# A Conformer-convolution and sparse-attention step on one core: first tile's projections feature by feature, samples' value products turned round, four square buffers

## The chip, the cores and the metric

The kernel runs on one core of a Trainium2 chip. The metric is the device time of one launch, in microseconds (us); the time before is the median of three runs. A core has TensorE (PE; its weight loads are shown as PEld), VectorE (DVE), ScalarE (ACT), GpSimd (POOL) and SyncE (SP, which issues the transfers), each with its own instruction stream, and they meet through semaphores. TensorE writes to PSUM, which has eight banks of 512 fp32 values per partition.

## What is computed

Two layers with a final RMSNorm, for 512 prompt tokens and 8 samples of 4 new tokens each (544 tokens in all, model width 1024).

```python
# layer 0: convolution mixer (width 2048, 31 taps per channel)
h = rms_norm(x, norm_g[0])
a, gl, z = split(h @ w_in, 3)
v = a * sigmoid(gl)
c = silu(layer_norm(depthwise_conv(concat(buf, v), dw_w) + dw_b))
x = x + (c * silu(z)) @ w_out
# layer 1: attention with three branches (compressed, selected, window), ALiBi slopes
q, z, kv, gates = split(rms_norm(x, norm_g[1]) @ w_in)
for each branch: o += gate * softmax(q k^T * scale - slope * distance) v
x = x + (o * silu(z)) @ w_out
y = rms_norm(x, final_norm_g)
```

A sample attends to 256 past tokens (pages for the selected branch, a window buffer for the window branch), to the compressed blocks of them, and to the new tokens.

## The kernel before, in words

**Layout.** Activations are feature-major: feature on the partitions, 544 tokens along the row; X holds eight such slices of 128 features. An fp32 product is split: weights and activations are each cut into a rounded high part (ScalarE's copy to fp32r) and the rest (a subtraction on VectorE or GpSimd), and `split_product` (L563) adds high x high, high x low and low x high, each over two column halves of 256 and 288: six matmuls.

**Opening.** ScalarE squares the eight slices of x, TensorE sums them with a matrix of ones, VectorE forms the inverse root, and `spread` (L549) spreads it over all partitions into banks 0 to 3, one quarter of the tokens in each. VectorE multiplies slice k by it (L1263, counted by h_ready); ScalarE copies the high part Hh (L1036, h1h_ready); VectorE subtracts to get Xl (L1267, h1l_ready). Meanwhile ScalarE copies and GpSimd subtracts the three weight blocks of tile 0 (`high_wA` L1028, `low_wA` L1703). TensorE waits for all eight h_ready (L608), since its first results go to banks 0 and 1, from which VectorE still reads.

**Convolution, 16 tiles of 128 channels.** `tile` on TensorE (L597): project the gate, add the taps of the tile before (`add_taps`, L586), project the linear part, project z. ScalarE takes the sigmoid from PSUM and prepares the next tile's high weights; VectorE multiplies into VP and runs 19 of the 31 taps; SP writes four shifted copies of VP to G (`spread_taps`, L437), from which TensorE adds the other 12 as products with diagonal matrices that GpSimd makes; GpSimd also does the samples' convolution and subtracts the weights. In the last tile TensorE takes 24 taps, and VectorE 7.

**Normalisation and output product.** After the last tile TensorE sums C over the channels, VectorE centres the 16 slices (L1329), ScalarE squares them into two buffers (L1083), TensorE sums (L627). Then, in a pipeline: VectorE scales, ScalarE applies SiLU, GpSimd multiplies with silu(z) (L1737), ScalarE and VectorE split the result, and TensorE adds blocks 0 and 1 of the output slice by slice (L644). Blocks 2 to 7 follow one by one. Of the output weights ScalarE copies the high parts (L1077, `high_wC` L1086); GpSimd subtracts for blocks 0 and 1 (L1732), VectorE for 2 to 7 (`low_wC`, L1347). Block 2's copy and subtraction stand after the pipeline.

**Attention.** Key, value, query and gate projections, the prompt's attention, then the samples' (L958 to L974): a loop of 16 steps, in each of which TensorE computes scores of unit v (`sample_scores`, L888: 32 columns of queries as weights, each sample's keys moving), transposes the weights of unit v-2, multiplies with the values for unit v-3 (`sample_pv`, L920) and does a quarter of a block of the prompt's output product (`out2`, 2 matmuls of 512 columns). There are 12 units: 4 of the compressed and 4 of the selected branch, alternating, then 4 of the window. In `sample_pv` the values (128x128) are the weights and 32 columns of attention weights move, one product for each sample and each half of its keys, so that the result is feature-major; the sum over branches lies in OS, and `sample_gate` (L1613) multiplies it into ZT. Every fp32 matmul shows as two records in the trace. After the loop come output blocks 4 to 7 and the final norm.

Each engine's order is written out by hand; a wait blocks all that follows on its engine.

## Time and profile before

| what | value |
|---|---|
| median of three runs | 1059.06 us (1058.37 to 1059.90) |
| the profiled execution's own time | 1058.09 us |
| its span in the trace | 1056.0 us |
| TensorE busy | 986.1 us, 93% |
| VectorE, ScalarE, GpSimd busy | 649.7, 404.6, 386.6 us |

The profile names a source line and tiles for every instruction. "Idle before" is the time that an engine stood still ahead of an instruction, with what ended the wait. The chain is followed back from the last instruction to what released each step. A busy TensorE need not run at full speed: the granted clock (PEclk) is 1.00 at 2.4 GHz and 0.50 at 1.2 GHz.

### The profile page before, as it was taken

Reading aid. Unit: us, or ns where it says so; the run is one execution under the profiler, and the core shown is the slowest. Engines: PE = TensorE matmul, PEld = TensorE weight load, DVE = VectorE, ACT = ScalarE, POOL = GpSimd, SP = SyncE. Lnnn points to the kernel's source line nnn. Section 1 sums busy time; section 2 is a strip of 40 time slices with the busy share of each in tenths; the row PEclk is TensorE's granted clock in tenths of the full one; section 3 lists DMA queues with packets and bytes.
Section 4 is the critical chain, followed back from the end, with each engine's and each line's share of the span. In section 5 each row is a group of like instructions: output and inputs, shape, how many; then the busy total and the mean of one; then the engine's idle time right before and its main releaser. Section 6 shows DMA issues by size and latency. Waiting matters only on the chain.

```text
span 1056.0 us, 19270 instructions
## 1 busy us (share of the span) xinstructions
PE 986.1 (93%) x7168; PEld 836.4 (79%) x7168; DVE 649.7 (62%) x1399; ACT 404.6 (38%) x794; POOL 386.6 (37%) x328
## 2 busy tenths in 40 slices
PE   2999999999999959999899998999699999999996
PEld 0989998998899729998799678999577777756684
DVE  4498999899989679320751312344888888833103
ACT  5333334333334276221331111244577777711001
POOL 2487888788878658001010000000333333100000
PEclk9999999999999959999899999998799999999796
DMA  8243453355334450360255015211630000260002
GB/s 342 75 128 101 127 174 103 101 139 163 101 105 137 139 202 1 120 238 7 115 152 133 1 26 221 80 61 41 205 124 1 0 1 1 104 235 1 1 1 85
DMA packets 43016, 108.01 MB, mean 102 GB/s; under 512 B 20674, under 2 KB 21730, under 8 KB 38530
## 3 DMA queue, kind: packets, MB, share of 16 engines
q1 hardware_dynamic: 42946, 106.99, 31.2%
q8 instruction: 54, 0.88, 0.3%
q14 instruction: 16, 0.13, 0.0%
HBM read 81.87 MB, written 12.17 MB: 89 GB/s over the span
## 4 chain that ended last, share of the span: by engine, by line
PE 82%; DVE 7%; issue 4%; ACT 4%; POOL 3%; DMA 0%; DVEq 0%; ACTq 0%
PE ps L567 52%; PE ps L953 7%; PE ps L593 4%; PE ps L843 4%; POOL C L1737 3%; PE ps L731 2%; PE ps L831 2%; PE ps L939 1%; PE ps L545 1%; DVE SX L1527 1%; DVE KL L1496 1%; PE ps L820 1%; PE ps L795 1%; DVE X L1263 1%; PE ps L822 1%
## 5 line engine op out<-in xcount | busy, mean ns | idle before, releaser
L567 PE MATMUL ps<-Hh,ringAh 128*128 128x256 f32 (+1 forms) x768 | 161.2, 291 | 14.3 <-DVE X L1263 14.3
L567 PE MATMUL ps<-Hh,ringAl 128*128 128x256 f32 (+1 forms) x768 | 159.4, 289 | 0.0
L1307 DVE SCALAR_TENSOR_TENSOR acc<-VP,tapc,acc 128x512 f32<-128x512 f32 x122 | 159.1, 1304 | 0.0
L567 PE MATMUL ps<-Xl,ringAh 128*128 128x256 f32 (+1 forms) x768 | 158.1, 287 | 0.0
L1706 POOL TENSOR_TENSOR ringAl<-ringA,ringAh 128x1024 fp32r<-128x1024 f32 x48 | 121.1, 2535 | 73.3 <-ACT ringAh L1029 73.2
L567 PEld LDWEIGHTS ps<-Hh,ringAh 128*128 128x128 f32 x768 | 123.3, 189 | 27.2 <-DVE X L1263 14.6
L567 PEld LDWEIGHTS ps<-Xl,ringAh 128*128 128x128 f32 x768 | 124.1, 189 | 0.0
L567 PEld LDWEIGHTS ps<-Hh,ringAl 128*128 128x128 f32 x768 | 123.0, 189 | 0.0
L1307 DVE SCALAR_TENSOR_TENSOR ps<-VP,tapc,ps 128x512 f32<-128x512 f32 x138 | 102.8, 745 | 0.6
L843 PE MATMUL ps<-PTB,V 128*128 128x512 f32 (+3 forms) x256 | 91.0, 439 | 2.5 <-ACT PTB L1206 2.1
L567 PE MATMUL ps<-Hh,ringEh 128*128 128x256 f32 (+1 forms) x384 | 84.2, 302 | 7.1 <-DVE ringEl L1373 4.6
L1029 ACT ACTIVATE ringAh<-ringA 128x1024 fp32r<-128x1024 f32 x48 | 50.7, 1060 | 87.9 <-PE ps L567 83.4
L567 PE MATMUL ps<-Hh,ringEl 128*128 128x256 f32 (+1 forms) x384 | 82.5, 298 | 0.0
L567 PEld LDWEIGHTS ps<-Hh,ringEh 128*128 128x128 f32 x384 | 64.9, 199 | 8.1 <-issue 8.0
L1373 DVE TENSOR_TENSOR ringEl<-ringE,ringEh 128x1024 fp32r<-128x1024 f32 x22 | 27.4, 1248 | 67.8 <-ACT ringEh L1112 67.7
L567 PEld LDWEIGHTS ps<-Hh,ringEl 128*128 128x128 f32 x384 | 64.7, 198 | 0.0
L1773 POOL CAST QS<-QT 64x512 fp32r (+1 forms) x16 | 10.1, 629 | 146.1 <-PE ps L822 82.6
L1678 POOL TENSOR_TENSOR prod<-VS,tapc 128x248 f32<-128x248 f32 x64 | 62.1, 1006 | 3.5 <-DVE VS L1292 3.5
L567 PE MATMUL ps<-Ch,ringCh 128*128 128x256 f32 (+1 forms) x256 | 54.9, 296 | 6.5 <-ACT Ch L1099 5.1
L1684 POOL TENSOR_TENSOR prod<-prod 128x512 f32<-128x512 f32 (+1 forms) x64 | 57.7, 901 | 5.0
L1206 ACT ACTIVATE PTB<-ps 128x128 f32<-128x128 f32 (+3 forms) x128 | 53.9, 421 | 9.9 <-PE ps L831 9.9
L843 PEld LDWEIGHTS ps<-PTB,V 128*128 128x128 f32 x256 | 44.0, 188 | 16.0 <-ACT PTB L1206 8.9
(233 smaller groups left out, 2059.6 us busy)
## 6 DMA issues: line engine op xcount, KB each, us to landing
ringA<-in_w_a SPq DMA_DIRECT2D x16, 1536.0 KB, 7.3
G<-VP SPq DMA_DIRECT2D x60, 260.0 KB, 4.8
ringE<-in_w_f SPq DMA_DIRECT2D x24, 512.0 KB, 3.6
ringC<-in_w_c SPq DMA_DIRECT2D x8, 1024.0 KB, 5.9
cache_cmp<-in_cache_cmp SPq DMA_DIRECT2D x32, 128.0 KB, 2.8
cache_sel<-in_cache_sel SPq DMA_DIRECT2D x16, 256.0 KB, 3.0
cache_win<-in_cache_win SPq DMA_DIRECT2D x1, 4096.0 KB, 15.2
out_win_s<-in_win_state SPq DMA_DIRECT2D x1, 4032.0 KB, 18.1
```

Source lines behind the costliest of these rows:

```text
L567: mm = nc.tensor.matmul(dst, w, x[:, cols], start=begins, stop=ends)
L593: mm = nc.tensor.matmul(ps[32 * j:32 * j + 32, 6], d[:, j, :], G[:, j, NSH * q:NSH * q + NP_], start=(q == 0), stop=(q == len(diags) - 1))
L843: mm = nc.tensor.matmul(out[:, P * k:NP_], V[:, k, v:v + P], PTB[:, b, k, P * k:NP_], start=False, stop=(b == 1 and k == 3))
L953: mm = nc.tensor.matmul(dst, w_o(n)[:, k, :], ZT[:, k, cols], start=(k == 0), stop=(k == KT - 1))
L1029: nc.scalar.activation(ringAh[:, j], ringA[:, par, j], ACT.Copy).then_inc(wAh_ready, 1)
L1206: nc.scalar.activation(PTB[:, turn, 0:t + 1, P * t:P * t + P], ps[:, 4 + u % 2, 0:(t + 1) * P].rearrange("p (k q) -> p k q", q=P), ACT.Cop ...
L1307: nc.vector.scalar_tensor_tensor(tap_sum(k % 2), src, w, tap_sum(k % 2), ALU.mult, ALU.add).then_inc(conv_step, 1)
L1373: nc.vector.tensor_tensor(ringEl[:, n % 3], ringE[:, n % 3], ringEh[n % 2][:].bitcast(F32), ALU.subtract).then_inc(wEl_ready, 1)
L1678: op = nc.gpsimd.tensor_tensor(dst, win, w, ALU.mult)
L1684: nc.gpsimd.tensor_tensor(prod[:, 0:n, :], prod[:, 0:n, :], prod[:, n:2 * n, :], ALU.add).then_inc(pool_step, 1)
L1706: nc.gpsimd.tensor_tensor(ringAl[:, par, j], ringA[:, par, j], ringAh[:, j].bitcast(F32), ALU.subtract).then_inc(wAl_ready, 1)
L1737: nc.gpsimd.tensor_tensor(C[:, c, :], C[:, c, :], Z1[:, c, :], ALU.mult).then_inc(c_gated, 1)
```

## The change

- **First tile.** The inverse root is spread into banks 6 and 7, two quarters in each, with a wait between the two halves; VectorE reads it as two rows of 272. TensorE no longer waits for all of h_ready: for each feature slice, once its high and low parts are there, it takes the gate's and then the linear product; z follows as before. GpSimd's third weight subtraction waits for six slices of Xl.
- **Last tile.** Strips 2 and 3 of the shifted rows are issued by ScalarE's queue, ahead of its copy into acc; SP issues 0 and 1.
- **Normalisation.** Squares go to four buffers (sqc) in memory that VP and sig have left.
- **Output weights.** Block 2's copy and subtraction move to GpSimd, behind those of blocks 0 and 1.
- **Samples.** In the value products the attention weights (32 columns per sample) become the weights of the matmul and the values move (128 columns); four samples write to four groups of 32 PSUM rows. The new tokens' product is one matmul for all samples in either branch. OS then is token-major; `sample_turn` transposes each of its four tiles on TensorE, one per step from step 12 on, and `sample_gate` reads the result from PSUM.

The diff, without the declarations of the semaphores half_spread and os_t:

```diff
@@ -142,6 +142,7 @@
         Cl = at("Cl", [P, CT, T], G0, F32R)
+        sqc = at("sqc", [P, 4, T], RINGA + 2 * 3 * KT * P * 4 + 17408)
@@ -434,13 +437,13 @@
-            def spread_taps(c, par, ptaps=PTAPS):
+            def spread_taps(c, par, ptaps=PTAPS, strips=range(NCG)):
...
                 k0, width = TAPS - ptaps, NP_ + ptaps - NSH
-                for j in range(NCG):
+                for j in strips:
@@ -454,7 +457,7 @@
             spread_taps(CT - 2, 0)
-            spread_taps(CT - 1, 1, PTAPS_LAST)
+            spread_taps(CT - 1, 1, PTAPS_LAST, range(0, 2))
@@ -558,7 +561,16 @@
             pe.wait_ge(rstd_kept, 1)
-            spread(0, rstd4).then_inc(rstd_ready, 1)
+            for half in range(2):
+                for b in range(2):
+                    j = 2 * b + half
+                    mm = nc.tensor.matmul(ps[:, 6 + b, Q * half:Q * half + Q], ones[32 * j:32 * j + 1, :],
+                                          rstd4[32 * j:32 * j + 1, :], start=True, stop=True)
+                    if half == 0:
+                        mm.then_inc(half_spread, 1)
+                if half == 0:
+                    pe.wait_ge(half_spread, 2)
+            mm.then_inc(rstd_ready, 1)
@@ -570,9 +582,6 @@
                 for k in range(KT):
-                    if j == 0 and not reaches(c, 1):
-                        pe.wait_ge(h1h_ready, k + 1)
-                        pe.wait_ge(h1l_ready, k + 1)
@@ -605,8 +614,22 @@
                 project(c, par, 2, 2, z_done)
-            pe.wait_ge(h_ready, KT)
-            for c in range(CT):
+            def first_tile():
+                for k in range(KT):
+                    pe.wait_ge(h1h_ready, k + 1)
+                    pe.wait_ge(h1l_ready, k + 1)
+                    for j in range(2):
+                        if k == 0:
+                            pe.wait_ge(wAl_ready, j + 1)
+                        mm = split_product(halves(j), ringAh[:, j, k, :], ringAl[:, 0, j, k, :],
+                                           Hh[:, k, :], Xl[:, k, :], k == 0, k == KT - 1)
+                        if k == KT - 1:
+                            mm.then_inc(gate_done if j == 0 else lin_done, 1)
+                project(0, 0, 2, 2, z_done)
+            first_tile()
+            for c in range(1, CT):
@@ -624,7 +647,7 @@
                 pe.wait_ge(squared, KT + c + 1)
-                add_up(0, sq[:, c % 2], c == 0, c == CT - 1).then_inc(sq_summed, 1)
+                add_up(0, sqc[:, c % 4], c == 0, c == CT - 1).then_inc(sq_summed, 1)
@@ -650,8 +673,10 @@
                 pe.wait_ge(wCh_ready, n + 1)
-                pe.wait_ge(wCl_ready, n - 1)
-                if n >= 3:
+                if n == 2:
+                    pe.wait_ge(wCl_first, 3)
+                else:
+                    pe.wait_ge(wCl_ready, n - 2)
@@ -926,25 +951,27 @@
                 out = ps[:, 4 + m % 2]
+                if m >= 6:
+                    pe.wait_ge(og_sample, m - 5)
                 if br == 0:
-                    nc.tensor.matmul(out[:, 0:P], vcs[:, gp * P:(gp + 1) * P], PT[:, v % 2, 0:P],
+                    nc.tensor.matmul(out[:, 0:P], PT[:, v % 2, 0:P], vcs[:, gp * P:(gp + 1) * P],
...
                 vnew = (br - 1) * GROUPS * HD + gp * P
-                for q in range(4):
-                    s_, cols = 4 * sg + q, slice(32 * q, 32 * q + 32)
-                    for c in range(2):
+                for c in range(2):
+                    for q in range(4):
+                        s_ = 4 * sg + q
...
                                 else cache_win[:, s_, (2 + c) * PAST + gp * P:(2 + c) * PAST + gp * P + P])
-                        nc.tensor.matmul(out[:, cols], vals, PT[:, v % 2, P * c + 32 * q:P * c + 32 * q + 32],
+                        nc.tensor.matmul(out[32 * q:32 * q + 32, 0:P], PT[:, v % 2, P * c + 32 * q:P * c + 32 * q + 32], vals,
                                          start=(br == 2 and c == 0), stop=False)
-                    if br == 2:
-                        mm = nc.tensor.matmul(out[:, cols], V[0:NS_, 4, vnew:vnew + P],
-                                              PT[0:NS_, v % 2, PAST + 32 * q:PAST + 32 * q + 32], start=False, stop=True)
-                if br == 1:
-                    mm = nc.tensor.matmul(out[:, 0:P], V[0:NS_, 4, vnew:vnew + P], PT[0:NS_, v % 2, PAST:PAST + P],
-                                          start=False, stop=True)
-                mm.then_inc(ss_pv, 1)
+                nc.tensor.matmul(out[:, 0:P], PT[0:NS_, v % 2, PAST:PAST + P], V[0:NS_, 4, vnew:vnew + P],
+                                 start=False, stop=True).then_inc(ss_pv, 1)
+            def sample_turn(w):
+                pe.wait_ge(os_kept, w + 5)
+                nc.tensor.transpose(ps[:, 4 + w % 2, P:2 * P], OS[:, w], ident[:]).then_inc(os_t, 1)
@@ -963,6 +990,8 @@
                     sample_pv(v - 3)
+                if v - 4 >= SAMPLE_WIN:
+                    sample_turn(v - 4 - SAMPLE_WIN)
@@ -1049,6 +1078,13 @@
                     high_wA(1 - par, 1)
+                if next_turn is None:
+                    act.wait_ge(v_ready, 2 * c + 1)
+                    act.wait_ge(taps_done, c)
+                    width = NP_ + PTAPS_LAST - NSH
+                    for j in range(2, NCG):
+                        src = VP[32 * j:32 * j + 32, par, TAPS - PTAPS_LAST:TAPS - PTAPS_LAST + width]
+                        act.dma_start(G[:, j, 0:width], windows(src, width)).then_inc(g_in, 16)
@@ -1078,12 +1114,14 @@
                 act.wait_ge(centered, c + 1)
-                if c >= 2:
-                    act.wait_ge(sq_summed, KT + c - 1)
-                nc.scalar.activation(sq[:, c % 2, :], C[:, c, :], ACT.Square).then_inc(squared, 1)
+                if c >= 4:
+                    act.wait_ge(sq_summed, KT + c - 3)
+                nc.scalar.activation(sqc[:, c % 4, :], C[:, c, :], ACT.Square).then_inc(squared, 1)
...
             def high_wC(n):
+                if n == 3:
+                    act.wait_ge(wCl_first, 3)
@@ -1111,7 +1149,6 @@
-            high_wC(2)
@@ -1270,7 +1307,9 @@
             for k in range(KT):
-                normalized(X[:, k, :], X[:, k, :], gains[:, 0, k:k + 1], ps[:, 0:4, 0:Q]).then_inc(h_ready, 1)
+                x2 = X[:, k, :].rearrange("p (b t) -> p b t", b=2)
+                nc.vector.scalar_tensor_tensor(x2, x2, gains[:, 0, k:k + 1], ps[:, 6:8, 0:2 * Q],
+                                               ALU.mult, ALU.mult).then_inc(h_ready, 1)
@@ -1349,7 +1388,6 @@
-            low_wC(2)
@@ -1613,10 +1651,10 @@
                 gp, sg = divmod(w, 2)
-                dve.wait_ge(os_kept, w + 5)
+                dve.wait_ge(os_t, w + 1)
...
                     rows = slice(HD * r, HD * r + HD)
-                    o4 = OS[rows, w].rearrange("p (s r j t) -> p r j s t", s=4, r=2, j=HPG)
+                    o4 = ps[rows, 4 + w % 2, P:2 * P].rearrange("p (s r j t) -> p r j s t", s=4, r=2, j=HPG)
@@ -1713,8 +1751,10 @@
-            for j in range(3):
-                low_wA(0, 0, j)
+            low_wA(0, 0, 0)
+            low_wA(0, 0, 1)
+            pool.wait_ge(h1l_ready, KT - 2)
+            low_wA(0, 0, 2)
@@ -1727,8 +1767,12 @@
-            for n in range(2):
-                pool.wait_ge(wCh_ready, n + 1)
+            for n in range(3):
+                pool.wait_ge(wCh_ready, min(n + 1, 2))
+                if n == 2:
+                    pool.wait_ge(wC_in[2], 16)
+                    nc.gpsimd.tensor_copy(ringCh[2][:], ringC[:, 2]).then_inc(wCh_ready, 1)
+                    pool.wait_ge(wCh_ready, 3)
```

## Rows read from the trace of the kernel before

**Rows 1.** The page: the chain that ended last, shares of the span by engine
```profile
PE 82%; DVE 7%; issue 4%; ACT 4%; POOL 3%; DMA 0%; DVEq 0%; ACTq 0%
```
**Rows 2.** Timeline of the opening: start us, us, engine, line, out<-in, [idle before <-releaser]
```profile
14.02 7.45 POOL L1706 TENSOR_TENSOR ringAl<-ringA,ringAh 128x1024 fp32r<-128x1024 f32 x3 [13.56 <-ACT ringAh L1029]
16.35 2.92 DVE L1267 TENSOR_TENSOR Xl<-X,Hh 128x544 fp32r<-128x544 f32 x1 [0.99 <-ACT Hh L1036]
...
23.30 0.77 DVE L1263 SCALAR_TENSOR_TENSOR X<-X,gains,ps 128x544 f32<-128x544 f32 x1
23.99 0.71 DVE L1267 TENSOR_TENSOR Xl<-X,Hh 128x544 fp32r<-128x544 f32 x1
...
28.10 0.82 PE L567 MATMUL ps<-Hh,ringAh 128*128 128x256 f32 x2 [14.28 <-DVE X L1263]
```
**Rows 3.** Busy time (x instructions) of PE, PEld, DVE, ACT, POOL; PEclk, DMA share, GB/s
```profile
28.10:33.00 4.90, 4.90 (x21) 4.90 (x22) 1.40 (x3) 0.64 (x1) 0.00 (x0) 1.00 0.00 0
33.00:42.50 9.50, 9.50 (x78) 9.50 (x77) 0.00 (x0) 2.92 (x4) 2.40 (x1) 1.00 0.01 2
```
**Rows 4.** Timeline after the first gate: table load, first copy and subtraction for tile 1
```profile
36.65 1.28 ACT L1044 ACT_TABLE_LOAD   x1 [7.91 <-PE ps L567]
...
38.51 1.06 ACT L1029 ACTIVATE ringAh<-ringA 128x1024 fp32r<-128x1024 f32 x1
...
39.74 2.40 POOL L1706 TENSOR_TENSOR ringAl<-ringA,ringAh 128x1024 fp32r<-128x1024 f32 x1 [18.27 <-ACT ringAh L1029]
```
**Rows 5.** Timeline of the last tile: issue of the shifted rows, taps, VectorE behind them
```profile
356.36 4.21 SPq L445 DMA_DIRECT2D G<-VP  x4
...
364.34 5.36 PE L593 MATMUL ps<-G,diag_last 128*32 128x512 f32 x48 [0.57 <-issue]
...
369.82 0.69 DVE L1310 TENSOR_TENSOR acc<-acc,ps 128x512 f32<-128x512 f32 x1 [8.49 <-PE ps L593]
```
**Rows 6.** Timeline of the normalisation: centring, one pair of squares, one of sums, the variance
```profile
372.89 10.19 DVE L1329 TENSOR_TENSOR C<-C,ps 128x544 f32<-128x544 f32 x16 [0.72 <-PE ps L552]
...
375.30 1.21 ACT L1083 ACTIVATE sq<-C 128x544 f32<-128x544 f32 x2 [0.37 <-PE ps L545]
...
377.53 1.24 PE L545 MATMUL ps<-sq,ones 128*32 128x136 f32 x16 [0.28 <-ACT sq L1083]
...
386.43 0.30 DVE L1256 TENSOR_SCALAR rstd<-ps 128x136 f32<-128x136 f32 x1 [3.36 <-PE ps L545]
```
**Rows 7.** Output weights: timeline rows, and from the page GpSimd's one kind of cast
```profile
369.64 9.08 POOL L1732 TENSOR_TENSOR ringCl<-ringC,ringCh 128x2048 fp32r<-128x2048 f32 x2 [5.73 <-ACT ringCh L1077]
...
390.75 1.34 POOL L1737 TENSOR_TENSOR C<-C,Z 128x544 f32<-128x544 f32 x1 [12.03 <-ACT C L1095]
...
423.54 0.49 PE L567 MATMUL ps<-Ch,ringCh 128*128 128x256 f32 x2 [1.00 <-DVE ringCl L1349]
...
428.66 2.29 DVE L1349 TENSOR_TENSOR ringCl<-ringC,ringCh 128x2048 fp32r<-128x2048 f32 x1 [5.26 <-ACT ringCh L1090]
...
L1773 POOL CAST QS<-QT 64x512 fp32r (+1 forms) x16 | 10.1, 629 | 146.1 <-PE ps L822 82.6
```
**Rows 8.** The chain between 924 and 1000: shares by line; pieces: start us, us, what
```profile
by line: PE ps L953 46.1%; PE ps L939 20.8%; PE ps L942 7.5%; PE ps L904 6.1%; PE ps L915 5.4%; PE ps L843 4.6%; PE ps L945 2.2%; PE ps L917 1.4%; PE ps L900 1.4%; PE ps L930 1.2%; PE ps L831 1.0%; DVE ZT L1540 0.9%; ACT PTB L1206 0.8%; PE 
...
931.59 0.58 PE ps L904 x8
...
932.24 1.91 PE ps L953 x4
...
940.17 1.71 PE ps L939 x16
941.88 0.41 PE ps L945 x2
```
**Rows 9.** Busy time and granted clock in the samples' stage, columns as in rows 3
```profile
929.00:971.00 42.00, 41.82 (x320) 25.12 (x320) 18.07 (x80) 6.99 (x24) 0.00 (x0) 1.00 0.29 119
971.00:1000.00 29.00, 29.00 (x108) 19.20 (x109) 5.16 (x20) 0.00 (x0) 0.00 (x0) 0.71 0.00 1
```

More of the change, by code:

```diff
@@ L274, in build @@
         rstd_ready = sem("rstd_ready")
+        half_spread = sem("half_spread")
         one_set = sem("one_set")
@@ L383, in build @@
         os_kept = sem("os_kept")
+        os_t = sem("os_t")
         og_sample = sem("og_sample")
```

## The prediction

> **What bounds the kernel now.** I read the page first: TensorE holds 82% of the chain of work that ended last, and no other engine more than 7%, so time is won only where TensorE waits, runs at half clock, or does work that another layout makes shorter [rows 1]. Then I read the stages that the diff touches, each in the timeline. In the **opening**, TensorE stands still for 14.28 us until the last of eight features is normalised, although the first one's two halves exist at 16.35 + 2.92 = 19.27 [rows 2]. In the **last tile** it waits 0.57 us for shifted rows [rows 5]; in the **normalisation** ScalarE squares in pairs and waits for TensorE's sums after each pair [rows 6]; before the third output block it waits 1.00 us for weights [rows 7]. In the **samples' stage** the chain is TensorE alone, and the value products (L939, L942) hold 20.8 + 7.5 = 28.3% of 76 us [rows 8]; the granted clock is 1.00 up to 971 and 0.71 after it, that is, it changes between 2.4 and 1.2 GHz [rows 9].
>
> **First tile, feature by feature.** The wait for all of h_ready goes, because the spread factors move to banks 6 and 7. TensorE can start at 19.27 instead of 28.10, 8.8 us earlier. Is it then fed? Per feature it does two split products, 12 records. A record takes 4.90/21 = 0.233 us in the first 4.9 us and 9.50/78 = 0.122 us after that [rows 3] (the PEclk column reads 1.00 for both; I go by the records), so a feature takes 2.8, later 1.46 us. VectorE makes a feature in at most 0.77 + 0.71 = 1.48 us when GpSimd is silent [rows 2], and TensorE has fallen two features behind by the time it is fast. So the 96 records run without a gap and both projections end about 33.7 instead of 42.5: I take 8.8 us. The 0.71 us subtraction took 2.92 us beside GpSimd [rows 2]; the diff puts GpSimd's third subtraction behind feature 5, where it can hold VectorE up for about 2.2 us twice: at worst a gap of 1.8 us. At best there is no slow stretch: 96 x 0.122 = 11.7 us instead of 14.4, 2.6 us more. Bounds 7.0 to 11.4. The wait between the two halves of the spread is covered by ScalarE's weight copies, which hold the first Xl until 16.35 anyway (without that cover: one more matmul latency, a few tenths).
>
> What is late next: the gate now ends with the linear part, so the sigmoid, with its 1.28 us table load, starts near 33.0, only 3.7 us earlier than now. From there to the end of GpSimd's first subtraction for tile 1 it takes 39.74 + 2.40 - 36.65 = 5.5 us [rows 4]: 38.5, against 33.7 + 48 x 0.122 = 39.6 for the end of tile 0. The sigmoid is done 38.51 - 36.65 = 1.9 us after the gate, at 34.9; VectorE's product needs under 0.8 us, and the shifted rows come 364.34 - 356.36 = 8.0 us after the start of their issue [rows 5]: 43.7, before the taps' turn at 39.6 + 5.9 = 45.5. Both reserves are 1 to 2 us; one missed costs about 1 us, inside the bounds.
>
> **Last tile.** Two of four transfers go to ScalarE's queue. Four take SP 4.21 us to issue; two by two they are out 2.1 us earlier, more than the 0.57 us that TensorE waits: 0.6 us (0 to 0.6). ScalarE's copy into acc comes 2.1 us later and so does VectorE's chain; cover is the 8.49 us that VectorE then waits for the taps [rows 5].
>
> **Four square buffers.** Now a pair of squares takes ScalarE 1.21 us, and up to 0.37 us of waiting follows; VectorE delivers a centred tile per 10.19/16 = 0.637 us. ScalarE and TensorE's sums (1.24 us a pair) could both go at 0.62, so VectorE becomes the pace: it ends at 383.08, then come a square of 0.61, a sum of 0.62 and the handing over, about 0.2: 384.5 against 386.43 [rows 6]. I take 1.9 us (0 if the pace stays, 2.2 at most).
>
> **Third block's weights to GpSimd.** Gone are the copy on ScalarE and the subtraction on VectorE ahead of the third block: the 1.00 us wait [rows 7]. GpSimd does a copy (0.629 us for 512 elements, so 2.5 for 2048, an estimate) and a third subtraction of 4.54 us after its two, 369.64 + 9.08 + 7.1 = 385.8. Its first gating product comes at 390.75 now and near 388.3 then, so 2.5 us of reserve cover it; at subtraction's pace for the copy 0.4 us is left. What is late next is the fourth block's weights, ready at 430.95, needed at 422.5 + 96 x 0.122 = 434.2. I take 1.0 us (0 to 1.1).
>
> **Samples' value products turned round.** Now a unit of the selected branch takes 1.71 + 0.41 = 2.12 us, four times [rows 8]. L939 and L942 hold 28.3% of 76 us = 21.5 us; less 4 x 1.71 that leaves 14.7 us for the four window units, 3.7 each. In the new order a unit is eight products with 32 columns of weights and 128 moving, four to a group of PSUM rows, and one full product for the new tokens. The nearest row is the scores' own shape: 16 records of 256 and 32 moving columns (L904 with L905) between 931.59 and 932.24, 0.65 us. Sixteen records of 128 columns are slightly fewer columns: 0.64, plus 0.41 as L945 has it: 1.05 us. Bounds: 0.6 if the groups overlap fully, 2.12 if the order of loads holds it as today. Gain: 4 x (2.12 - 1.05) + 14.7 - 4 x 1.05 = 14.8 us, less four new transposes (L915 holds 5.4% of 76 us in 20 of them, 0.2 each): 14.0. VectorE has 18.07 us of work in those first 42 [rows 9], under half, and its copies fall under the 1.91 us of output product in each unit, so TensorE stays the bound; gating out of PSUM instead of SBUF costs nothing on the path, since an output product lies between turn and use.
>
> **The clock there.** A quarter of an output block takes 1.91 us at full clock [rows 8]. L953 holds 46.1% of 76 = 35.0 us for 62 records, which at 1.91 for four are 29.6: 5.4 us are lost at 1.2 GHz up to 1000, and about 0.5 more after it and in the transposes: 5.9. The clock fell while TensorE ran the 3.7 us window units of 32 moving columns, and rose and fell again with each. Units after the change look like those of 929 to 971, which ran at 1.00 throughout; I take it that the clock stays up: 5.9 us (0 to 5.9).
>
> **Waits added.** TensorE's wait for os_kept before each turn finds VectorE's sum an output product old; its wait for og_sample before window units 2 and 3 asks for gates that end about 1 us after a turn, again an output product earlier. ScalarE's waits for v_ready and taps_done ahead of its two transfers are met together with the wait for v_ready that stands there now; behind them stand the acc copy (above) and the SiLU of the last z, not due before the tile ends. GpSimd's wait for h1l_ready holds back only the third subtraction, needed at 33.7 and done near 28.5. Its wait for the third load holds back the gating products, counted above.
>
> **Sum.** 8.8 + 0.6 + 1.9 + 1.0 + 14.0 + 5.9 = 32.2 us. The profiled execution took 1058.09 us (span 1056.0), 0.97 under the median of 1059.06: 1025.9 for it, 1026.9 for the median.
>
> **Rivals.**
> *The clock still falls in the last units.* Each still has its transposes and small products between output products. Then 5.9 us come back: 1033. For it: the fall in the same units now; against it: those units are 2.7 us shorter, and the selected units, which are nearer in shape, did not lower it. 12%.
> *Turned units stay load- or switch-bound.* They switch between 32-column weights and full ones, twice more per unit. Two records of L945 take 0.41 us where two of 128 columns would take 2 x 0.107 = 0.21 by L939's pace, so a switch shows about 0.2 us. A unit at 2.12 us gives 8 x 1.07 = 8.6 back: 1035.5. Against it: the scores switch twelve times in the chain, and pay little. The Trainium skill (TensorEngine Tiling (Array Packing), Key Properties) says that a change of tiling mode drains TensorE and names no time; by that rule the units would pay two drains each. By the 0.2 us seen, 16 drains are 3.2 us, of which one per unit is already in the 1.05. 9%.
> *Slower: the clock stays at 1.2 GHz from the first turned unit on.* Place: from 940.2 to the end of the loop [rows 8, 9]; that is 60 us now and 60 - 19.9 = 40 us after the change at full clock, 80 at half. It gives 1027 + 40 = 1067. It decides if over 32 of those 40 us run at half clock. For it: the clock does fall in this loop, in units of small products; against it: 42 us of the same loop at 1.00 with score products of just this shape. 2%.
> *The change doesn't do what it says in the conv half*: squares still paced by something else, tile 1 waits for its sigmoid and weights, GpSimd late. Worth 1.9 + 1.0 + 1.8 + 1 back at most: 1033. 10%.
>
> **How the numbers follow.** The forecast has 67%, its own range 1023.5 to 1031. The range must reach to the first, second and fourth rival: 1023 to 1036; below lie a fast start and faster units together. Some 0.2% is what a measurement of this kernel can tell from no change; every case but the third rival lies far below that: faster 0.96, same 0.01, slower 0.03.
>
> **What would show it.** Right: TensorE's first product near 19.3 and tile 0's linear part done near 33.7, then tiles of the same length; no pairs in the squares; no TensorE wait before the third block; value units near 1.05 us and a granted clock of 1.00 until the loop ends. Wrong: gaps in the first 96 records, a granted clock of 0.50 in the last units, turned units of 2 us, or VectorE named as what TensorE waits for there.

## The result, and the profile after

The changed kernel took **1023.7 us** (1023.41 to 1024.97), beside 1059.48 us (1058.37 to 1067.49) for the kernel before on the same chip. The ratio is **0.9646 [0.9601, 0.9692]**; on the 1059.06 us that the forecast started from, that is 1021.6 us (1016.8 to 1026.4). The forecast was 1026.9, its range 1023 to 1036: the direction and the main mechanisms were right, and the gain came out larger than the range allowed. Three of the four executions before are the ones that the forecast started from (1058.37 to 1059.90), and the fourth took 1067.49. Against the first three alone the median of 1023.7 us lies just inside the range; with the fourth the gain lies 1.4 us outside it. The profiled execution took 1023.85 us (span 1022.0), 34.2 us less than the profiled 1058.09; 32.2 had been added up.

The page of the kernel after, the chain that ended last, by engine:

```profile
PE 82%; DVE 7%; issue 4%; ACT 3%; POOL 3%; DMA 0%; DVEq 0%; ACTq 0%
```

TensorE still holds 82% of the chain [rows 1]: the bound has not moved to another engine. Where the time went is read stage by stage, from positions in the two traces.

**Opening.** The timeline of the kernel after, rows that answer to [rows 2 to 4]:

```profile
16.45 2.92 DVE L1304 TENSOR_TENSOR Xl<-X,Hh 128x544 fp32r<-128x544 f32 x1
...
19.47 0.79 PE L579 MATMUL ps<-Hh,ringAh 128*128 128x256 f32 x2 [4.65 <-DVE Xl L1304]
...
26.09 2.41 POOL L1744 TENSOR_TENSOR ringAl<-ringA,ringAh 128x1024 fp32r<-128x1024 f32 x1 [7.29 <-DVE Xl L1304]
26.62 3.09 DVE L1304 TENSOR_TENSOR Xl<-X,Hh 128x544 fp32r<-128x544 f32 x2
...
33.33 1.28 ACT L1073 ACT_TABLE_LOAD   x1 [5.94 <-PE ps L579]
...
45.90 2.78 PE L602 MATMUL ps<-G,diag 128*32 128x512 f32 x24
```

TensorE's wait of 14.28 us became 4.65. Up to the second tile's taps no other row of TensorE has an idle time: no gap. GpSimd's held-back subtraction does lengthen a low part: the last two take 3.09 us together, where each takes 0.71 alone. But TensorE is some three features behind by then. The wait between the two halves of the spread delays VectorE's first slice by 0.9 us (14.87 instead of 13.89, with the inverse root 0.1 later), and the first low part only by the 0.1 (16.45 instead of 16.35): it is covered, as forecast. The first taps start at 45.90 instead of 54.45: 8.55 us.

**Last tile and normalisation.** The timeline of the kernel after, rows that answer to [rows 5 to 7]:

```profile
347.81 1.19 SPq L448 DMA_DIRECT2D G<-VP  x2
347.82 2.46 ACTq L1087 DMA_DIRECT2D G<-VP  x2
...
355.04 5.33 PE L602 MATMUL ps<-G,diag_last 128*32 128x512 f32 x48
...
363.57 10.19 DVE L1368 TENSOR_TENSOR C<-C,ps 128x544 f32<-128x544 f32 x16 [0.72 <-PE ps L555]
364.39 10.07 ACT L1119 ACTIVATE sqc<-C 128x544 f32<-128x544 f32 x16 [0.43 <-DVE C L1368]
365.19 7.91 PE L548 MATMUL ps<-sqc,ones 128*32 128x136 f32 x104 [1.67 <-ACT sqc L1119]
370.59 1.88 POOL L1774 CAST ringCh<-ringC 128x2048 fp32r<-128x2048 f32 x1
372.55 4.55 POOL L1776 TENSOR_TENSOR ringCl<-ringC,ringCh 128x2048 fp32r<-128x2048 f32 x1
...
375.02 0.30 DVE L1293 TENSOR_SCALAR rstd<-ps 128x136 f32<-128x136 f32 x1 [1.26 <-PE ps L548]
```

The wait ahead of the last taps is gone (364.34 to 355.04: 0.75 us more). The squares are one group of 16 now, not eight pairs with idle time between them, and end 0.7 us after the centring; the variance comes at 375.02 instead of 386.43, 2.1 us more. GpSimd's copy and subtraction end at 377.1, before its first gating product. When the next stage's first product starts (505.25 before, 492.98 after), the conv half has won 12.27 us; 8.8 + 0.6 + 1.9 + 1.0 = 12.3 had been forecast. From there to the samples' loop 0.6 us are lost again (424.94 us instead of 424.36), a loss that the three small parts come back to.

**Samples' loop.** Busy time and granted clock, columns as in [rows 3], first of the kernel before over the whole loop, from the first block of output products to the fifth:

```profile
929.61:1000.89 71.28, 71.28 (x421) 44.51 (x422) 22.68 (x99) 6.99 (x24) 0.00 (x0) 0.88 0.16 67
```

and of the kernel after, the loop, the next three blocks with the first half of the samples' output product, and the end:

```profile
917.92:967.20 49.28, 49.28 (x400) 24.69 (x401) 22.56 (x99) 7.00 (x24) 0.00 (x0) 1.00 0.22 95
967.20:994.00 26.80, 26.80 (x141) 23.04 (x139) 3.06 (x7) 1.97 (x3) 0.00 (x0) 1.00 0.01 1
994.00:1009.00 15.00, 15.00 (x69) 12.56 (x69) 0.29 (x1) 2.29 (x4) 0.00 (x0) 0.66 0.00 0
```

71.28 became 49.28: 22.0 us, with the clock at 1.00 to the end of the loop. An old window unit in the timeline of the kernel before (a quarter of the unit; the other three lie in between), and the output product behind it:

```profile
985.17 0.60 PE L939 MATMUL ps<-PT,cache_win 128*128 128x32 f32 x4
985.70 0.40 PE L942 MATMUL ps<-PT,V 32*128 32x32 f32 x2
...
988.72 3.67 PE L953 MATMUL ps<-ZT,WOq 128*128 128x512 f32 x4
```

That unit takes 3.55 us, and the output product behind it 3.5 us (to 992.23), where a quarter at full clock takes 1.8. A turned unit in the timeline of the kernel after, and a turn behind the next unit:

```profile
953.01 0.65 PE L966 MATMUL ps<-cache_win,PT 128*32 128x128 f32 x16
953.59 0.48 PE L968 MATMUL ps<-V,PT 32*128 32x128 f32 x2
954.00 1.98 PE L980 MATMUL ps<-ZT,WOq 128*128 128x512 f32 x4
...
957.23 0.33 PE L974 MATMUL ps<-ident,OS 128*128 128x128 f32 x1
```

From start to start a turned unit is 0.58 + 0.41 = 0.99 us, and a turn 0.17 (to 957.40). Note the first two columns: L966 starts at 953.01 and is busy for 0.65, but L968 starts at 953.59. Busy times of neighbouring groups overlap by 0.07; they cannot be added up.

**Tail.** Here no part of the change is at work, and the clock falls. Timeline of the kernel before, then of the kernel after:

```profile
1022.89 10.61 PE L953 MATMUL ps<-ZT,WOq 128*128 128x32 f32 x64
...
1034.49 8.59 PE L953 MATMUL ps<-ZT,ringE 128*128 128x256 f32 x32
```

```profile
989.20 9.34 PE L980 MATMUL ps<-ZT,WOq 128*128 128x32 f32 x64
998.47 1.14 PE L548 MATMUL ps<-sq,ones 128*32 128x136 f32 x16
999.54 9.90 PE L980 MATMUL ps<-ZT,ringE 128*128 128x256 f32 x32
```

The products of 32 moving columns took 1.3 us less and the last block 1.3 us more: the same fall of the clock (0.66 in the mean from 994 on), met a little later. All in all, 12.27 - 0.6 + 22.0 + 0.3 for the end give the 34.0 us by which the two spans differ.

### The profile page after: what moved, and what is told of

It reads as the page before. It is cut to its first block, busy times and chain, and to the rows that moved or that the text cites. A ratio compares the mean times of both kernels' runs of the same rounds, so it can differ in the third digit from the quotient of the medians.

```text
span 1022.0 us, 19230 instructions
## 1 busy us (share of the span) xinstructions
PE 964.4 (94%) x7148; PEld 816.7 (80%) x7148; DVE 648.7 (63%) x1398; ACT 403.5 (39%) x793; POOL 392.7 (38%) x330
## 4 chain that ended last, share of the span: by engine, by line
PE 82%; DVE 7%; issue 4%; ACT 3%; POOL 3%; DMA 0%; DVEq 0%; ACTq 0%
PE ps L579 54%; PE ps L980 7%; PE ps L602 4%; PE ps L868 4%; POOL C L1781 3%; PE ps L756 3%; PE ps L856 2%; DVE SX L1565 1%; DVE KL L1534 1%; PE ps L548 1%; DVE C L1368 1%; PE ps L845 1%; PE ps L820 1%; PE ps L847 1%; PE ps L864 1%
```

## The experiments

Positions below are starts on TensorE. "The loop" is the stretch just shown. The kernel before took from 1052.95 to 1067.82 us over all 35 executions that stand beside this study, so its own spread is wider than most parts of the change; the parts are read from the traces. Each kernel has one trace, so a stretch that varies from execution to execution is seen once in each.

### The two halves of the change by themselves

The samples' part alone: the hunks of the diff on the value products, the turns, the waits for og_sample and os_t, and the gate out of PSUM.

> Only the samples' part of the change: value products turned round, four turns on TensorE, gating out of PSUM; the conv half stays as before. Theory A (the samples' loop alone is worth what the two traces show, 22.0 us between the starts of the first and the fifth output block, and the tail gives nothing): 22 us less than before, about 1037, loop 49.3 us, granted clock 1.00 in it. Rival B (the 19.9 us of the forecast were right, the other 2 us come with the conv half, because weights and cache rows arrive earlier against the loop): 20 us less, about 1039, loop 51.4 us.

The rest alone: all other hunks.

> The conv half of the change alone: first tile feature by feature, last tile's strips on two queues, four square buffers, third block's weights on GpSimd; the samples' stage stays as before. Theory A (parts add up): 12 us less than before, about 1047, the samples' loop 71.3 us long as before, granted clock falling in its last units. Rival B (2 us of the loop's gain belong to this half): 14 us less, about 1045, and a loop of 69 us.

Measured: 1037.03 us (1034.65 to 1038.45), ratio 0.9761 [0.9698, 0.9824], for the samples' part; 1048.51 (1046.22 to 1054.61), ratio 0.9881 [0.9809, 0.9953], for the rest. The ratios multiply to 0.9645, where the whole has 0.9646; with intervals of 0.7% on each side, so close an agreement is chance, and the parts are read from the loop. The loop of the samples' part alone, busy time of TensorE, granted clock, DMA share, GB/s:

```profile
930.10:979.38 49.28, 49.28 (x400) 1.00 0.24 98
```

and of the rest alone, cut where its clock falls:

```profile
919.30:962.00 42.70, 42.70 (x325) 1.00 0.28 113
962.00:992.00 30.00, 30.00 (x101) 0.66 0.00 1
```

Theory A holds for the loop: 49.28 us, as in the kernel after, the full 22.0. Rival B asked for a shorter loop with the rest alone; it was longer, 72.70, because the clock fell lower. The same old loop took 71.28, 71.33, 71.34, 69.75 and 72.70 us in five profiles, the turned one 49.28 in three. The stage ahead of it also varies: from the first product of KS and QS (prompt attention) to the first output product of the loop it took 177.3 us in seven of the twelve profiles and 178.4 to 179.0 in five, in kernels with the change and without, so these 1.1 us and more are not the change's.

### The opening alone, and without the held-back subtraction

The opening alone is the first tile, the spread in banks 6 and 7, and GpSimd's wait; the second kernel then takes the wait away:

```diff
             low_wA(0, 0, 1)
-            pool.wait_ge(h1l_ready, KT - 2)
             low_wA(0, 0, 2)
```

> The opening alone: first tile's two projections feature by feature, spread factors in banks 6 and 7, GpSimd's third subtraction held back until VectorE's sixth low part. Theory A: the taps of the second tile start 8.6 us earlier, none of it given back before the samples: 8.6 us less, about 1050.5. Rival B (a shorter opening moves later stages onto loads that then come late): some of it lost after tile 1, 7 us less or fewer.

> As the opening alone, but GpSimd's third subtraction is not held back: it follows the first two at once, beside VectorE's low parts. Theory A (the two engines slow each other: a low part took 2.92 us beside GpSimd and 0.71 alone): at least two low parts take over 1.5 us in the first half of the tile, TensorE gets a gap of 1 to 2 us, and the second tile's taps start 0 to 2 us later than with the delay; about 1051 to 1052. Rival B (TensorE is behind by more than that, or GpSimd's third subtraction ends before VectorE matters): no difference to the opening alone, within 0.3 us.

Measured: 1048.81 us (1047.19 to 1050.25), 0.9868 [0.9805, 0.9930], and 1048.97 us (1045.49 to 1051.53), 0.9877 [0.9809, 0.9944]. First taps at 44.68 and 44.96, 9.8 and 9.5 us earlier than in the kernel before. At the samples' loop 7.6 and 9.0 us of that are left. The opening alone loses 1.1 us ahead of the last taps, where TensorE's wait grew from 0.57 us [rows 5] to 1.69. Another 1.0 us goes between the next stage's first product and the first product of KS and QS. So "none of it given back" fell in that execution, as rival B has it, though not down to its 7 us. The wait ahead of the last taps differs from execution to execution: it was 0.40 to 0.57 us in five of the six profiles in which SP issues all four strips, and 1.69 in this one. The timeline without GpSimd's wait:

```profile
18.54 2.86 POOL L1729 TENSOR_TENSOR ringAl<-ringA,ringAh 128x1024 fp32r<-128x1024 f32 x1
...
19.77 2.20 DVE L1288 TENSOR_TENSOR Xl<-X,Hh 128x544 fp32r<-128x544 f32 x1
19.85 0.66 PE L577 MATMUL ps<-Xl,ringAh 128*128 128x256 f32 x2
```

The contention is there, 2.20 us for a low part that takes 0.71 alone. Beyond the very first low part, which takes 2.92 us with the held-back subtraction and without, it is only this one, and it ends at 21.97, just as TensorE finishes the first feature's twelve records (19.26 + 12 x 0.23 = 22.0). Theory A's gap did not appear; rival B's limit of 0.3 us held. Against the kernel after, both runs have the first taps about 1 us earlier, because TensorE's records changed from 0.23 to 0.12 us sooner (four or five groups earlier). That change has no fixed place: from the first product to the first taps it took 25.4 to 26.8 us in the twelve profiles, in the old order of the first tile or the new.

### The three small parts

Four square buffers, strips on two queues, third block's weights on GpSimd.

> The four square buffers, the two strips on ScalarE's queue and the third block's weights on GpSimd, without the opening and the samples. Theory A (the three are worth what the two traces show, 0.7 + 2.1 + 1.2 us, up to the fourth block of the conv half's output product, and no more of it is lost before the samples than the run-to-run spread of that stretch, 1.8 us): the last tile's taps to the start of the second block of products 27.7 us apart instead of 29.8, granted clock falling in the old samples' loop, 69 to 79 us long. Rival B (what the untouched middle gave back is the price of GpSimd's later work): the middle is longer than in the kernel before by 0.9 us or more.

Measured: 1055.51 us, in one execution. The last tile's taps start at 364.19 and the first output product of the conv half at 391.85, 27.66 us apart (29.77 before): theory A. (The expectation called that first output product the second block of products by mistake; the two numbers in it belong to the first.) The next stage's first product comes 110.26 us later, instead of 111.14: the third block's 0.9 us.

From there to the loop, where nothing was changed, it took 425.17 us against 424.36, 0.8 us more, close to rival B's 0.9. Most kernels agree: up to the first product of KS and QS this stretch takes 247.6 to 247.9 us in all six kernels with the three small parts, and 246.4 to 247.0 in five of the six others. The sixth, the opening alone, has 247.9 too, so it can come without them. Some 0.6 to 0.8 us of what the small parts win thus seems to be given back there. Whether GpSimd's later work does it, as rival B says, is not shown.

### The old value products in two pieces

In the four window units of the kernel before, an output product goes between two samples' value products and the other two's:

```diff
-                if 3 <= v < 15:
+                window = SAMPLE_WIN <= v - 3 < 12
+                if 3 <= v < 15 and not window:
                     sample_pv(v - 3)
...
-                mm = out2(n, range(2 * quarter, 2 * quarter + 2), [(ps[:, 6 + n % 2], slice(0, NP_))])
+                for k in range(2 * quarter, 2 * quarter + 2):
+                    if window:
+                        sample_pv(v - 3, (range(0, 2), range(2, 4))[k % 2])
+                    mm = out2(n, [k], [(ps[:, 6 + n % 2], slice(0, NP_))])
```

> The kernel before with one thing moved: in the four window units, and the three places after them, nothing of the work changes, but each window unit's value products are cut in two (two samples each) and one of the two full-width output products of that place goes after each half. Theory A (the old loop loses time to the clock because each window unit runs some 3.7 us of 32-column products in one piece): granted clock 1.00 through the loop, loop 64.5 to 66 us instead of 71.3, 5 to 7 us less in all, about 1052. Rival B (the clock follows the share of such products over the whole stretch, not the unbroken piece): it still falls, loop 69 to 73 us, no clear change.

Measured: 1064.8 us (1059.21 to 1067.43), 1.0041 [1.0000, 1.0082]. The loop, cut where the clock falls, and the timeline at that place:

```profile
929.29:977.00 47.71, 47.71 (x343) 1.00 0.24 97
977.00:1003.24 26.24, 26.24 (x78) 0.54 0.00 1
```

```profile
976.14 1.13 PE L955 MATMUL ps<-ZT,WOq 128*128 128x512 f32 x2
977.10 0.53 PE L940 MATMUL ps<-PT,cache_win 128*128 128x32 f32 x4
...
979.20 2.08 PE L955 MATMUL ps<-ZT,WOq 128*128 128x512 f32 x2
```

Theory A fell. With full-width products in between, the clock still falls (the same two records of the output product take 1.13 us and then 2.08), and it stays low until the units are over: 0.54 in the mean over the last 26 us. The kernel before had 0.71 over its last 29 [rows 9], but each is one execution, so the difference proves nothing; the ten executions of this kernel lie within the range of those of the kernel before. Spreading the old products out in this way does not help.

### The old value products in the new order

Not turned; in the selected units one half of all four samples goes first, then the other:

```diff
-                for q in range(4):
-                    s_, cols = 4 * sg + q, slice(32 * q, 32 * q + 32)
-                    for c in range(2):
+                for i in range(8):
+                    q, c = (i % 4, i // 4) if br == 1 else (i // 2, i % 2)
...
```

> The kernel before, not turned, with the selected units' value products in the order of the kernel after (one half of all four samples, then the other). Theory A (each of the eight products pays a full weight load ahead of 32 moving columns, whatever the order): 1.71 us for the 16 records as before. Rival B (the second half of a sample waits for the first, which adds into the same columns): 1.3 us or less, 1.6 us less in all over four units.

Measured: 1065.88 us, in one execution; unit and loop:

```profile
940.40 1.87 PE L940 MATMUL ps<-PT,cache_sel 128*128 128x32 f32 x16
942.20 0.48 PE L946 MATMUL ps<-PT,V 32*128 32x128 f32 x2
```

```profile
930.00:972.00 42.00, 42.00 (x320) 1.00 0.29 114
972.00:1008.68 36.68, 36.68 (x107) 0.53 0.00 0
```

1.80 us from start to start, as in the kernel before (7.19 us for four): theory A's number. The order is worth nothing; that a weight load is what these products pay for is not shown by it. The loop took 78.68 us, with window units that were not touched: the clock went down right behind the first of them (in the kernel before, within it) and had a mean of 0.53 over the last 36.7 us. So the old samples' stage can bring an execution to 1066.

### The turned products, order and number

First the two loops exchanged, so that consecutive products go to the same rows of PSUM:

```diff
-                for c in range(2):
-                    for q in range(4):
+                for q in range(4):
+                    for c in range(2):
```

> The kernel after with the two loops of the turned value products exchanged: both halves of one sample right after each other, into the same group of 32 rows of PSUM, instead of one half of all four samples first. Theory A (the four groups run side by side because consecutive products go to different groups): the 16 records of a unit take 0.8 to 1.1 us instead of 0.57, 8 units, so a loop of 51 to 53.5 us and 1026 to 1028. Rival B (the gain is the short weight load of 32 columns alone): 0.57 us as now, loop 49.3 us, 1023.7.

Measured: 1024.04 us (1022.18 to 1025.28), 0.9666 [0.9601, 0.9730], loop 49.45 us. A unit of it:

```profile
953.40 0.66 PE L966 MATMUL ps<-cache_win,PT 128*32 128x128 f32 x16
953.99 0.48 PE L968 MATMUL ps<-V,PT 32*128 32x128 f32 x2
```

0.59 us from start to start instead of 0.58: rival B's number. The gain does not hang on the order; whether the short weight load alone makes it is for the next run to say. Then each window unit's eight products six times over (REPEATS is 6):

```diff
-                for c in range(2):
+                for i in range(2 * (REPEATS if br == 2 else 1)):
+                    c = i % 2
...
-                                         start=(br == 2 and c == 0), stop=False)
+                                         start=(br == 2 and i == 0), stop=False)
```

> The kernel after, with the eight turned value products of each of the four window units run six times over instead of once (the window values are summed six times, so the outputs of the samples are not the reference's): 48 products, 96 records, about 3.5 us per unit, as long as the window units of the kernel before. Theory A (it is the shape that lowers the clock: one 32-column product after another, not the time between two full-width output products): granted clock stays 1.00, each unit costs five times 0.58 us more, the loop is 49.3 + 4 x 2.9 = 60.9 us and the time about 1035, with a spread of 2 to 4 us as after. Rival B (any such piece of small products of over 3 us lowers it): the granted clock falls to 0.50 in the last units as before, loop 66 to 75 us, 1041 or more.

Measured: 1033.89 us (1032.26 to 1035.2), 0.9717 [0.9661, 0.9773]. A unit with the scores ahead of it, and the whole loop:

```profile
952.02 0.66 PE L932 MATMUL ps<-cache_win,qblk 128*32 128x256 f32 x8
952.47 0.27 PE L933 MATMUL ps<-KTm,qblk 128*32 128x32 f32 x8
...
953.14 2.83 PE L970 MATMUL ps<-cache_win,PT 128*32 128x128 f32 x96
955.90 0.48 PE L972 MATMUL ps<-V,PT 32*128 32x128 f32 x2
956.32 1.98 PE L984 MATMUL ps<-ZT,WOq 128*128 128x512 f32 x4
```

```profile
918.05:976.07 58.02, 58.02 (x721) 1.00 0.19 81
```

Theory A: the clock stays at 1.00 through pieces of 2.76 + 0.41 us, nearly as long as the old units (3.55 us at full clock), where it fell. It is not the share of such products either: they fill 12.7 of the 19.4 us from 953.14 to the end of the last unit, two thirds, and the cut old products filled 5.9 of 9.1 us, two thirds too, when the clock fell at 977.9. So neither the length of the piece between two output products nor its share decides, but the form of the products. What in that form does it, these runs do not separate.

The size was off: five more passes cost 2.76 - 0.58 = 2.18 us, 0.44 each and not 0.58, so a pass runs at 0.027 us per record once it is under way. A quarter of an output block, four records of 512 columns, takes 1.83 us from start to start, so full-width products move 128 columns in 1.83 / 16 = 0.114 us, about four times as long. The Trainium skill (TensorEngine Tiling (Array Packing), Key Properties and Theoretical Speedup) says that tiles of a mode load and multiply in parallel, up to four times the throughput where one dimension is 32 or less. This run lies at that bound: 0.114 / 0.027 = 4.2, or 3.9 with the shortest quarters of the loop, 1.72 us. The time goes with the columns, and is no fixed cost of a record: eight records of 256 columns of the scores, also behind 32 columns of weights, take 0.45 us, 0.057 each. So the short weight load, rival B's reason in the run with the loops exchanged, cannot be the whole gain: products of different groups run side by side, in either order.

### A version that takes the same step in the tail

The samples' output product of the first four blocks is the same kind of work: 32 moving columns behind full weights, 9.34 us, and the clock falls on it. Turned, with the samples' attention as weights (TensorE's part of the edit):

```diff
+                if n == 4:
+                    pe.wait_ge(x2_added, 4)
+                    for k in range(KT):
+                        j = k % 4
+                        mm = nc.tensor.matmul(ps[32 * j:32 * j + 32, 6, :].rearrange("p (m f) -> p m f", m=4),
+                                              ZT[:, k, NP_:T], WOq[:, :, k, :], start=(k < 4), stop=(k >= 4))
+                    mm.then_inc(turned_done, 1)
+                if n == 5:
+                    pe.wait_ge(turned_kept, 1)
+                    pe.wait_ge(stack2_in, 16)
+                    for m in range(4):
+                        mm = nc.tensor.matmul(ps[:, 6, NS_ * m:NS_ * m + NS_], S[:, 0, P * m:P * m + P], stack2[:],
+                                              start=True, stop=True)
+                    mm.then_inc(out2s_done, 1)
...
```

> The kernel after with the samples' output product of the first four blocks turned the same way: eight products with the samples' 32 columns of attention as weights and 512 moving columns of output weights, spread over four groups of 32 rows of PSUM after the fifth block; ScalarE copies the four partial sums out during the sixth block, and four products with four stacked identities as moving side add and turn them back; squares and sums of the first four blocks move ahead of the last block. Theory A (the 9.34 us of 32 records-wide products before the last block were load-bound and lowered the clock for the last block too): 2 to 3 us for the turned product, the granted clock stays 1.00 in the last block, which takes 7.4 us instead of 9.9: 8 to 10 us less than after, 1014 to 1016. Rival B (eight products of 512 columns don't run side by side): 7.5 us for them, 2 to 4 us less in all because of the clock, 1020 to 1022.

Measured: **1015.64 us** (1013.96 to 1017.32), 0.9586 [0.9537, 0.9635]; the kernel with the two loops exchanged, within 0.2 us of the kernel after in the profiles' loops, took 1024.04 on the same chip. The timeline:

```profile
975.78 1.92 PE L1039 MATMUL ps<-WOq,ZT 128*32 128x512 f32 x16
...
985.07 0.97 PE L1046 MATMUL ps<-stack,S 128*128 128x32 f32 x8
...
993.39 1.60 PE L554 MATMUL ps<-sq,ones 128*32 128x136 f32 x48
994.92 7.60 PE L986 MATMUL ps<-ZT,ringE 128*128 128x256 f32 x32
```

and the stretch from the loop's end to that of the last block:

```profile
968.35:1002.40 34.05, 34.05 (x201) 1.00 0.00 1
```

Theory A: 1.85 + 0.81 us instead of 9.27, and the last block 7.53 instead of 9.83 with the clock at 1.00. From the loop's end to that of the span it takes 46.8 us instead of 54.8: 8 us less than the kernel after. The moved squares and sums are part of this version and were not run by themselves.

## Why the prediction was wrong in size

**The step that failed is the samples' loop**, in the size of its two terms: 14.0 us for the value products and 5.9 for the clock, 19.9 in all, against 22.0. The mechanism was right. Adding the distances from start to start in the two timelines gives each term:

| work in the loop | before | after | won | forecast |
|---|---|---|---|---|
| value products, with the turns | 24.00 | 7.91 + 0.61 | 15.5 | 14.0 |
| output products | 35.85 | 29.34 | 6.5 | 5.4 |
| scores, transposes, the rest | 11.43 | 11.42 | 0.0 | 0.5 |

(The table goes by the kind of work, so the first line holds the clock's loss within the old window units, about 0.9 us: they took 15.15 us in all, and 4 x 3.55 = 14.2 at full clock. The last line includes the compressed branch's own value products, 0.9 us on either side.) Three readings made up the difference. The old products were taken from the chain's shares, 21.5 us for L939 and L942, where the distances give 22.3: 0.8 us. The new unit was put at 1.05 and is 0.99, a turn at 0.20 and is 0.15: 0.7 together. The 1.05 came from a slip in scaling: the row taken, 0.65 us for 8 x 256 + 8 x 32 = 2304 columns, gives 0.58 for 16 x 128 = 2048, not 0.64, and 0.58 is what was measured. And the full-clock quarter was taken as 1.91 us, the longest kind of piece in the chain (others are 1.72), where 29.34 / 16 = 1.83 is the mean: 1.1 us of clock loss unseen, less the 0.5 that was added for the transposes, which won nothing.

**The second failure is the kernel before's own clock loss.** The forecast took one execution's loss as the kernel's, and added 0.97 for the median. But that loss is drawn anew in each execution: old loops of 69.75 to 72.70 us, and 78.68 with the order changed in units ahead of it. The 35 executions of the kernel before have a median of 1060.1 and fall into two groups: 18 from 1052.95 to 1060.11, none in the next 4.7 us, and 17 from 1064.82 to 1067.82. Where their mean granted clock is on record, it is 0.952 to 0.960 in the first group and 0.945 to 0.948 in the second. What draws the group is open. The turned loop has no such loss (49.28 us in each of three profiles) and the four executions of the kernel after lie within 1.6 us, so no offset was to be carried over: its profiled execution, 1023.85, is within 0.15 of its median.

So the loop's 2.1 us and the offset's 0.97 lead from 1026.9 to the measured median of 1023.7, near enough. The 2.1 us from there to 1021.6 are the fourth execution of the kernel before, of the second group. The range's low end, "a fast start and faster units together", allowed 3.9 us below the forecast; the term whose bound was wrong is the clock's "5.9 us (0 to 5.9)", which took the one profile's loss for the most there could be. The "0.2%" that a measurement was said to tell from no change fell with it: the kernel before alone spans 1.4%.

**Opening**: 8.8 forecast, 8.55 measured; TensorE started at 19.47 and not at 19.27. "TensorE has fallen two features behind by the time it is fast" held; GpSimd's third subtraction held VectorE up once and not twice, and its price, a gap of up to 1.8 us, was nothing, held back or not. The gate's table load started at 33.33 (33.0 forecast), and the second tile's start did not wait for it.

**Last tile, squares, third block**: 0.75, 2.1 and 0.9 us against 0.6, 1.9 and 1.0. The 0.57 us wait behind the first of them differs between executions too, as the opening alone shows. VectorE's centring became the pace, as argued, and GpSimd's copy took 1.88 us, under the 2.5 estimated, which left 2.2 us to its gating products.

**The rivals.** The clock that still falls in the last units: no, 1.00 throughout. Turned units bound by loads or switches: no, 0.99 us. The new-token product still takes 0.41 us for two records, where the compressed branch's two of 128 columns take 0.22, so the 0.2 us put down to a switch are still there. The Trainium skill (TensorEngine Tiling (Array Packing), Key Properties) says that a change of tiling mode drains TensorE. That the 0.2 us are this drain is not shown, since the product also has only 32 rows and adds to columns that were just written. The slower case, the clock at 1.2 GHz from the first turned unit on: no, and the run with six passes shows how far from it the turned units are. The conv half not doing what it says: no, 12.27 of 12.3 at its end, less the 0.6 us lost behind it.

## What to carry to other kernels

Where a product has 32 moving columns behind 128 columns of weights, swap its sides and spread it over four groups of PSUM rows: here a unit of eight fell from 2.2 us (selected) or 3.8 (window, part of it at the lower clock) to 0.99, and the clock loss around it went too. Add up distances from start to start, not busy times, when a stage has hundreds of short groups. A stretch whose granted clock was below 1.00 in a profile was one draw here: bound such a term by several executions, on both sides.

## What was not expected

The order of the turned products is worth 0.01 us a unit, although consecutive products then share their rows of PSUM: 0.59 against 0.58. Full-width products between the old ones did not hold the clock up; it stayed at 0.50 for 24 us. In the first tile's first records, the granted clock reads 1.00 while they take 0.23 us each, and the time from the first product to the first taps differs by 1.4 us from execution to execution with the place where they become 0.12; what sets it stays open here. What in the old products lets the clock fall also stays open: the runs exclude the length of the piece, its share of the time and the work between, and show that the turned form does not have it. The order within the old window units was not tried.
